# Norm borders that hand on x s + z g, sums inside the last output tile, and gates made in the branch stages, in a five-branch fp32 kernel

## The reference

```
h = rms_norm(x, norm_g); proj = h @ w_in            # z, xbc, dt, lru gate, lru x, q, gates
xbc = silu(causal_dwconv(xbc, conv_w, conv_b)); dt = softplus(dt_raw + dt_bias)
y_ssd = rms_norm((ssd_scan(xs, dt, -exp(a_log), b, c) + xs * d) * silu(z))
y_lru = rg_lru(causal_dwconv(lru_x)) * silu(lru_gate)
y_mem = memory_attention(q, rms_norm(mem), w_kv)
x = rms_norm(x + (gates0 * (y_ssd @ w0) + gates1 * (y_lru @ w1) + gates2 * (y_mem @ w2)) @ w_out, final_g)
for i, branch in enumerate((s5, swa, mla, sgu)):     # swa: 16 heads, window 128; mla: 16 heads, causal
    x = x + rms_norm(branch(rms_norm(x, pre_norm[i])), post_norm[i])
# s5, swa, mla:  (y * silu(z)) @ w_out, y a scan with GLU or an attention; sgu: (u * s * silu(z)) @ w_out
# s5 coefficients: dt = exp(log_dt), exp(lam_re dt), cos and sin of lam_im dt, and quotients of them
```

## Time and profile before

| | |
|---|---|
| device time, three runs | 2221.42, 2221.95, 2225.58 us (median 2221.95) |
| the profiled execution | 2225.19 us, of which the span is 2223.4 us |
| mean granted TensorE clock | 0.955 of full speed |
| PE busy | 2005.2 us, 90% of the span |
| DVE, ACT, POOL busy | 1293.1, 861.0, 455.7 us |
| data moved | 227.96 MB, mean 103 GB/s |

### The profile page before, as it was taken

One profiled execution on the slowest core, in us unless ns is written; L12 is line 12 of the kernel. 1 busy time (PEld: TensorE's weight loads), 2 busy tenths in 40 slices (PEclk: granted clock), 3 DMA queues, 4 the chain that ended last, 5 costly groups with the idle time before them and its releaser, 6 DMA issues.

```text
span 2223.4 us, 24707 instructions
## 1 busy us (share of the span) xinstructions
PE 2005.2 (90%) x9910; PEld 1569.7 (71%) x9910; DVE 1293.1 (58%) x1862; ACT 861.0 (39%) x1247; POOL 455.7 (20%) x386
## 2 busy tenths in 40 slices
PE   6897888999999999999999887989889988789986
PEld 4685765788667888778787765867667755468865
DVE  6986885725539235555537344475486456547374
ACT  4223646412268224322332342355442344444232
POOL 1864100323158403033300100012001010100001
PEclk9998998999999999999999998999999999999998
DMA  3244331234322534334465527211222210123211
GB/s 137 84 147 136 128 120 55 79 116 147 114 92 80 169 116 156 146 112 151 135 156 148 135 80 157 76 57 39 76 93 82 76 38 19 39 76 123 95 57 57
DMA packets 63938, 227.96 MB, mean 103 GB/s; under 512 B 13744, under 2 KB 30800, under 8 KB 43472
## 3 DMA queue, kind: packets, MB, share of 16 engines
q1 hardware_dynamic: 22896, 162.54, 20.9%
q0 software_dynamic: 20240, 48.58, 7.6%
q10 hardware_dynamic: 20688, 15.26, 3.1%
HBM read 208.72 MB, written 17.56 MB: 102 GB/s over the span
## 4 chain that ended last, share of the span: by engine, by line
PE 61%; DVE 11%; ACT 6%; issue 4%; DMA 2%; ACTq 1%; POOL 0%; DVEq 0%
PE bank L482 17%; PE bank L483 17%; PE bank L484 17%; PE bank L481 2%; DVE ring_low L444 1%; ACT ring_high L439 1%; PE bank L3142 1%; ACT swa_s L3046 1%; ACTq L2414 1%; PE bank L3169 1%; DMA ring<-slabs 1%; PE bank L1938 1%; DVE swa_s L2983 1%; DVE lru_x L1852 1%; PE bank L609 1%
## 5 line engine op out<-in xcount | busy, mean ns | idle before, releaser
L482 PE MATMUL bank<-h_high,ring_high 128*128 128x512 f32 x1248 | 508.5, 407 | 46.1 <-DVE h_low L1364 22.2
L444 DVE TENSOR_TENSOR ring_low<-ring,ring_high 128x2048 fp32r<-128x2048 f32 x136 | 329.4, 2423 | 352.8 <-ACT ring_high L439 352.7
L483 PE MATMUL bank<-h_low,ring_high 128*128 128x512 f32 x1248 | 495.3, 397 | 0.0
L484 PE MATMUL bank<-h_high,ring_low 128*128 128x512 f32 x1248 | 494.3, 396 | 0.0
L439 ACT ACTIVATE ring_high<-ring 128x2048 fp32r<-128x2048 f32 x145 | 277.3, 1913 | 518.5 <-PE bank L484 505.9
L482 PEld LDWEIGHTS bank<-h_high,ring_high 128*128 128x128 f32 x1248 | 240.7, 193 | 116.4 <-issue 52.4
L483 PEld LDWEIGHTS bank<-h_low,ring_high 128*128 128x128 f32 x1248 | 240.5, 193 | 53.4 <-issue 4.4
L484 PEld LDWEIGHTS bank<-h_high,ring_low 128*128 128x128 f32 x1248 | 239.8, 192 | 51.8
L482 PE MATMUL bank<-gated_high,ring_high 128*128 128x512 f32 x256 | 106.1, 415 | 25.1 <-issue 18.2
L444 POOL TENSOR_TENSOR ring_low<-ring,ring_high 128x2048 fp32r<-128x2048 f32 x9 | 43.2, 4805 | 366.5 <-ACT ring_high L439 366.5
L483 PE MATMUL bank<-gated_low,ring_high 128*128 128x512 f32 x256 | 103.7, 405 | 0.0
(11 more groups left out here) (519 smaller groups left out, 3807.5 us busy)
## 6 DMA issues: line engine op xcount, KB each, us to landing
ring<-slabs SPq DMA_DIRECT2D x149, 1024.0 KB, 4.8
acs_rows<-acs_rows POOLq DMA_DIRECT2D x16, 512.0 KB, 4.7
s_outputs<-s_ca POOLq DMA_DIRECT2D x4, 1152.0 KB, 7.2
x<-xT SPq DMA_DIRECT2D x2, 2048.0 KB, 8.8
exp_acs<-acs_rows POOLq DMA_DIRECT2D x16, 256.0 KB, 8.8
s_b<-s_br POOLq DMA_DIRECT2D x8, 512.0 KB, 4.3
s_rows<-s_powers POOLq DMA_DIRECT2D x16, 256.0 KB, 6.3
s_inputs<-s_w POOLq DMA_DIRECT2D x8, 512.0 KB, 3.0
```

Of the source, the lines that this page charges most:

```text
L444: dve.tensor_tensor(self.ring_low[:, s % RING, :], self.ring[:, s % RING, :], self.ring_high[:, self.splits_before[s] % AHEAD, :].bitcast( ...
L482: pe.matmul(out, w[0], x[0], start=start, stop=False)
L483: pe.matmul(out, w[0], x[1], start=False, stop=False)
L484: return pe.matmul(out, w[1], x[0], start=False, stop=stop)
```

## The change

- **Columns and coefficients.** The columns are loaded in three pieces, the 96 of the S5 coefficients first; `s5_coefficients` moves from `stage_xbc` into `stage_load`, ahead of the first squares on ACT and of the first sums on DVE.
- **dt's softplus** is cut in pieces at tiles 4, 8, 12 and 16 of `stage_xbc` (before: all at 4, the sums at 9), and ACT makes a slab's high part one tile earlier.
- **Sum in the tile.** The gathered squares of seven tiles are summed by a matmul at k = 5 of the last output tile; only the last square is summed behind it. At the first block's end the whole sum goes behind k = 2 of the S5 layer's first gemm.
- **Borders.** With s the root of z's mean square, the border hands on x s + z g, s being a factor for each token, and not x + z g / s. The next norm takes it out again (eps s^2 in its sum). The reciprocal and eight products that bring x back to size (`invert_on_dve`, `settle_on_dve`) come inside the next stage's entry. After the first block, whose norm has no add, the parts are made before the root.
- **Gates.** `Gate` makes silu(z), the product and both parts tile by tile inside the branch stages: in S5's GLU stage by a sigmoid, in SWA's and MLA's loops by 0.5 z (1 + tanh(z/2)), where DVE's product reads y from the bank instead of ACT's copy; in `stage_sgu` by silu and a product into u. In MLA the calls stand as in SWA, once for two heads.
- **SGU's output** does its first four tiles together, k outermost, with the blocks in that order.
- **The bias** goes to DRAM in 16 copies instead of 128 and is read back by eight skewed transfers.

```diff
+    add("sgu_out", [("d_w_out", span(k * P), span(m * P)) for k in range(KD) for m in range(4)])
+    for m in range(4, KD):
...
+    loaded, cols, s5_cols = C.reserve("loaded", 16), C.reserve("cols_loaded", 32), C.reserve("s5_cols_loaded", 16)
+    s5_act, s5_dve = s5_coefficients(C)
+    a = COL_AT["lam_re"]
+    own = slice(a, a + 96)
...
-            act.dma_start(C.cols[:], io["cols"]).then_inc(cols.sem, 16)
+            act.dma_start(C.cols[:, own], io["cols"][:, own]).then_inc(s5_cols.sem, 16)
+            act.dma_start(C.cols[:, 0:a], io["cols"][:, 0:a]).then_inc(cols.sem, 16)
+            act.dma_start(C.cols[:, a + 96:NCOL], io["cols"][:, a + 96:NCOL]).then_inc(cols.sem, 16)
+            act.wait_ge(s5_cols.sem, s5_cols.base + 16)
+            s5_act(act)
...
-            dve.wait_ge(cols.sem, cols.base + 16)
+            dve.wait_ge(s5_cols.sem, s5_cols.base + 16)
+            s5_dve(dve)
+            dve.wait_ge(cols.sem, cols.base + 32)
...
             def step_sums():
+                log1p_end(C, dve, L.S1[:], L.S2[:], L.S4[:])
...
                 if i == 4:
-                    step_sizes()
-                if i == 9:
+                    dve.wait_ge(dts.sem, dts.at(1))
+                    log1p_ratio(C, dve, L.S1[:], L.S2[:])
+                if i == 8:
+                    log1p_terms(C, dve, L.S2[:], L.S3[:], L.S4[:], 15, 9)
+                if i == 12:
+                    log1p_terms(C, dve, L.S2[:], L.S3[:], L.S4[:], 7, 3)
+                if i == 16:
...
-                if i >= 3:
-                    C.split_high(act, u)
+                if 3 <= i + 1 < len(tiles):
+                    C.split_high(act, tiles[i + 1][0])
...
+    def sum_gathered(self, pe):
         C, u, n = self.C, self.u, len(self.src)
         C.open(pe, u)
         pe.wait_ge(self.summed.sem, self.summed.at(n - 1 - self.split))
-        mm = pe.matmul(C.bank[u.b][:, 0:self.w], C.ones[:], self.total, start=True, stop=not self.split)
+        return pe.matmul(C.bank[u.b][:, 0:self.w], C.ones[:], self.total, start=True, stop=not self.split)
+    def sum_total(self, pe, gathered=False):
+        C, u, n = self.C, self.u, len(self.src)
+        if not gathered:
+            mm = self.sum_gathered(pe)
...
+        if last.add is not None:
+            self.last_root_on_act(act)
...
-            ins = dve.scalar_tensor_tensor(out=last.tmp[i], in0=last.src[i], scalar=last.g(i), in1=last.root, op0=ALU.mult, op1=ALU.mult)
+            if last.add is None:
+                dve.wait_ge(last.squared.sem, last.squared.at(i))
+                ins = dve.tensor_scalar(C.X[:, i, :], C.X[:, i, :], last.g(i), None, ALU.mult)
+            else:
+                dve.wait_ge(self.before.sem, self.before.at(i))
+                ins = dve.tensor_tensor(C.X[:, i, :], C.X[:, i, :], last.root, ALU.mult)
             ins.then_inc(last.scaled.sem, 1)
         def grow(i):
             if last.add is not None:
                 dve.wait_ge(last.scaled.sem, last.scaled.at(i))
-                dve.tensor_tensor(C.X[:, i, :], C.X[:, i, :], last.tmp[i], ALU.add).then_inc(self.grown.sem, 1)
+                dve.scalar_tensor_tensor(out=C.X[:, i, :], in0=last.src[i], scalar=last.g(i), in1=C.X[:, i, :], op0=ALU.mult,
+                                         op1=ALU.add).then_inc(self.grown.sem, 1)
...
-        C.vchain.link(dve, dve.reciprocal(last.root, last.root))
...
+        last = self.last
+        self.C.read(dve, last.u)
+        dve.scalar_tensor_tensor(out=self.total, in0=last.root, scalar=EPS * DM / P, in1=last.root, op0=ALU.mult, op1=ALU.mult)\
+            .then_inc(self.summed.sem, 1)
...
+    def invert_on_dve(self, dve):
+        dve.wait_ge(self.summed.sem, self.summed.at(0))
+        dve.reciprocal(self.last.root, self.last.root).then_inc(self.inverted.sem, 1)
+    def settle_on_dve(self, dve, i):
+        X = self.C.X[:, i, :]
+        dve.wait_ge(self.inverted.sem, self.inverted.at(0))
+        dve.wait_ge(self.lows.sem, self.lows.at(i))
+        dve.tensor_tensor(X, X, self.last.root, ALU.mult).then_inc(self.settled.sem, 1)
...
+                if i == 4:
+                    entry.invert_on_dve(dve)
+                for n in ({4: (0, 1, 2), 5: (3, 4, 5, 6, 7)} if stats else {4: (0,), 5: (1, 2), 6: (3, 4), 7: (5, 6, 7)}).get(i, ()):
+                    entry.settle_on_dve(dve, n)
...
+                        if k == 2:
+                            entry.last.sum_total(pe)
...
+            entry.invert_on_dve(dve)
+            for i in range(KD):
+                entry.settle_on_dve(dve, i)
...
+    def after_glu(act, i):
+        if i + 1 < KD:
+            gate.curve_on_act(act, i + 1, C.zbuf[:, i + 1, :], ACT.Sigmoid, 1.0)
+        if i > 0:
+            gate.high_on_act(act, i - 1)
+        if i == KD - 1:
+            gate.high_on_act(act, i)
     def glu_mul(dve, i):
         dve.tensor_tensor(Y[:, i, :], Y[:, i, :], L.Y[:, i, :], ALU.mult).then_inc(glu_made.sem, 1)
-    glu_tiles = stage_gemm(C, KD, L.G, glu, then=glu_mul, side=Side(ready=split))
+        gate.factor_on_dve(dve, i, C.zbuf[:, i, :], 0.0)
+        dve.wait_ge(glu_made.sem, glu_made.at(i))
+        dve.wait_ge(gate.factor.sem, gate.factor.at(i))
+        dve.tensor_tensor(Y[:, i, :], Y[:, i, :], C.zbuf[:, i, :], ALU.mult).then_inc(gate.mul.sem, 1)
+        if i > 0:
+            gate.low_on_dve(dve, i - 1)
...
+        self.slots = [C.root[:, 1, :]]
...
+    def curve_on_act(self, act, k, z, fn, scale):
+        if k > 0:
+            act.wait_ge(self.factor.sem, self.factor.at(k - 1))
+        act.activation(self.slots[0], z, fn, scale=scale).then_inc(self.curve.sem, 1)
+    def factor_on_dve(self, dve, k, z, plus):
+        dve.wait_ge(self.curve.sem, self.curve.at(k))
+        dve.scalar_tensor_tensor(out=z, in0=self.slots[0], scalar=plus, in1=z, op0=ALU.add, op1=ALU.mult).then_inc(self.factor.sem, 1)
+    def high_on_act(self, act, k):
+        act.wait_ge(self.mul.sem, self.mul.at(k))
+        act.activation(self.parts.high[:, k, :], self.Y[:, k, :], ACT.Copy).then_inc(self.high.sem, 1)
+    def low_on_dve(self, dve, k):
+        dve.wait_ge(self.high.sem, self.high.at(k))
+        dve.tensor_tensor(self.parts.low[:, k, :], self.Y[:, k, :], self.parts.high[:, k, :].bitcast(F32), ALU.subtract)\
+            .then_inc(self.low.sem, 1)
...
+            for u in us:
+                C.open(pe, u)
+            for k, row in enumerate(blocks):
+                pe.wait_ge(gate.low.sem, gate.low.at(k))
+                for u, (s, i) in zip(us, row):
+                    C.wait_slab(pe, s, seen)
+                    mm = C.product(pe, C.bank[u.b][:], C.block(s, i), gate.parts.tile(k), k == 0, k == KD - 1)
+                    if k == KD - 1:
+                        mm.then_inc(C.bank_full[u.b], 1)
...
+                if i >= together:
+                    ready = (lambda k: pe.wait_ge(gate.low.sem, gate.low.at(k))) if i == 0 else None
+                    if i == KD - 1:
+                        ready = lambda k: post.sum_gathered(pe) if k == 5 else None
+                    C.gemm(pe, t, gate.parts.tiles(KD), seen, ready=ready)
                 if i in side.tensor:
                     side.tensor[i](pe)
-            post.sum_total(pe)
+            post.sum_total(pe, gathered=True)
...
-        pool.dma_start(scr, L.BV[:].unsqueeze(1).to_broadcast([16, P, 384])).then_inc(s.sem, 16)
+        pool.dma_start(scr, L.BV[:].unsqueeze(1).to_broadcast([16, 16, 384])).then_inc(s.sem, 16)
         pool.wait_ge(s.sem, s.base + 16)
-        skewed = bass.AP(tensor=scr.tensor, offset=127, ap=[[383, P], [P * 384, 16], [1, 256]])
-        pool.dma_start(L.BT[:], skewed).then_inc(s.sem, 16)
+        for a in range(8):
+            skewed = bass.AP(tensor=scr.tensor, offset=127 - 16 * a, ap=[[383, 16], [16 * 384, 16], [1, 256]])
+            pool.dma_start(L.BT[16 * a:16 * a + 16], skewed).then_inc(s.sem, 16)
...
+            def gated(j):
+                u = ob[j]
+                C.full(dve, u)
+                dve.wait_ge(gate.factor.sem, gate.factor.at(j))
+                dve.scalar_tensor_tensor(out=L.Y[:, j, :], in0=C.bank[u.b][:], scalar=0.5, in1=L.Z[:, j, :], op0=ALU.mult,
+                                         op1=ALU.mult).then_inc(C.bank_read[u.b], 1)
+                C.read(dve, u)
+                dve.sem_inc(gate.mul.sem, 1)
...
+            gate.factor_on_dve(dve, 0, L.Z[:, 0, :], 1.0)
             for j in range(NJ):
                 if j + 1 < NJ:
                     probs(j + 1)
+                if j > 0:
+                    gated(j - 1)
                 if j + 2 < NJ:
                     logits(j + 2)
                     evac_z(j + 2)
+                if j + 1 < NJ:
+                    gate.factor_on_dve(dve, j + 1, L.Z[:, j + 1, :], 1.0)
+                if j > 1:
+                    gate.low_on_dve(dve, j - 2)
+            gated(NJ - 1)
+            for j in (NJ - 2, NJ - 1):
+                gate.low_on_dve(dve, j)
...
+            def curve(j):
```

(53 more changed lines are left out.)

182 lines of the change are left out of this document (101 added, 81 removed).

## The result

The changed kernel takes 2187.18 us (median of 4 runs, 2184.87 to 2193.54), the kernel before 2223.55 (4 runs): a ratio of 0.9841, interval 0.9817 to 0.9865, or 35 us less. The forecast was 2167, some 56 less. The time lies just inside the range of 2150 to 2188, but outside the 2155 to 2180 that had a chance of 0.62, and a third of the forecast gain is missing. The profiled execution took 2188.14 us, its span 2186.0; 37.4 less than the 2223.4 of before.

A forecast was written before the change was run, and what follows sets the result against it. PE, busy for 90% of the span, was taken as the bound, so only its idle time and the lower-clock matmuls after it could be won. The terms sum to -56.4, giving 2167 us; forecast 2155 to 2180, range 2150 to 2188.

The forecast's parts named there:

- Start: Kernel start: split columns load and early S5 coefficients delay PE's first sum, +7.5 us; ends +2 and +8.
- Convolution: First block's convolution and scan: dt's softplus in pieces and POOL's earlier chain remove PE's waits, -20.5 us.
- The other part of the term, the scan: Before the SSD scan: POOL's chain begins some 38 us earlier, so PE's wait of 9.71 goes, -9.4 us.
- its other bound: Convolution and scan: only part is won, -12 us, if POOL is slowed or slows the low halves.
- Border to S5 and S5's gate: First block to S5: reciprocal leaves the path, -6.1 us; S5's output stage starts with only the last k open, -7.6.
- MLA's entry: Entry of MLA: reciprocal and eight settling products, 8.9 us on DVE against 3 idle, +5.2 us; bounds 3 and 6.
- SGU: SGU's output: gate made earlier and first four tiles k-major, ending together near 2174.5, -6.5 us; bounds -4 and -8.
- Borders, gates, loops: Later borders -10.4, -2.6, -2.6; gates of S5, SWA, MLA -7.6, -8.0, -8.2; loops of SWA +6.1, MLA -3.5.
- The slower one: Head loops: DVE's new product waits for PE's attention product, loops run in series; +39, 2261 us; chance 0.03.
- The early landing: Kernel start: the first piece of columns lands early, making the start cheap; -62, 2161 us; chance 0.14.
- this rival: Head loops: tanh has its own table, two loads of 1.28 per 16 tiles, +41; -15, 2207 us; chance 0.02.
- the -34: SWA's and MLA's loops give back more, +25 against +2.6; total -34, 2189 us; chance 0.11, including table loads.

The follow-up runs named there:

- pool_held: The changed kernel with POOL's chain of S5 tables held until the 24th tile of the convolution is done; 2280.54 us.
- coef_back: The changed kernel with the S5 coefficients computed in the convolution's stage as before, columns still in three pieces; 2189.27 us, ratio 0.9849.
- glu_low: The changed kernel with the last low part of S5's gate ahead of the slab's low half, not behind it; 2179.97 us (one run).

## Why the forecast was wrong where it was

- **Start (+7.5, measured +8.2).** Right in mechanism and size: the piece landed at 8.6 and the squares began at 14.68. The Trainium skill (DMA: Bandwidth & Descriptors, Queues, rings and completion order) has the engines take turns between queues packet by packet. The trace agrees (205 packets on one queue and 190 on the other in 9 us). What does not hold is what the forecast drew from it, an early landing and +2 for "a piece with a third of the descriptors": the piece has as many packets as x, 144, and landed with it. What the forecast did not see is that the two other pieces would now hold DVE until 14 by themselves.
- **Convolution (-20.5, measured -12.8).** The step that failed is the sum of won waits, 1.2 + 8.7 + 2.5 + 1.0 less 2.3 for "a wait that I expect at a low half", -11.1. PE's last gemm matmul ahead of the scan (187.16 before, 195.20 after) is 8.0 us late, where the first was 8.2 late: 0.2 us were won. The wait of 8.74 fell to 2.61, but the new one is 5.43, not 2.3, and with the matmuls behind it at a granted clock of 0.64 (166 to 172 us; 1.00 there before) it took 7.5 back. The cover assumed for the pieces was the slack of a slab, 10.9 us of PE for 16 blocks. In fact DVE is busy all through, and POOL, brought forward by the same change, stretches DVE's steps (3.05 for 0.68). Shown by pool_held; coef_back agrees. The other part of the term, the scan, won 12.7 and not 9.4: its wait went, and the matmuls behind it, which ran at a granted clock of 0.52 (197 to 203 us), now have 1.00 (195 to 200), which the forecast left out. coef_back shows that the wait went because POOL's chain starts earlier (33 us, not the 38 of the forecast). The text had -12 as its other bound and chose the wrong end; that the total lies so near to -12 is luck, as neither part does.
- **Border to S5 and S5's gate (-13.7, measured -10.4).** In the gate the step "low(7)", which the working took as free, stood behind a slab's low half and cost 3.5 us (glu_low); without it the gate would have won 9.9, more than its 7.6. At the border PE's first S5 matmul won 5.1 us and the one at 1094.83 6.2, as forecast. Some 2 us are lost again up to 1252, in the part of the span where repeats differ; why was not tried.
- **MLA's entry (+5.2, measured +7.2).** The step was right (no idle time for 8.9 us of DVE), and PE's waits grew by 4.7, from 4.16 to 6.14 and 2.74. The size was off at the clock: the forecast took 0.7 off for it, but the matmuls in and behind the two waits cost 2.5 more (granted clock 0.59 from 1641 to 1654, 0.84 from 1664 to 1675 before).
- **SGU (-6.5, measured -0.4).** The step "k-major the first four end together" left out that four banks must be free. With them free 6.9 more are won.
- **Borders, gates, loops.** Each reciprocal, gate and loop term came out within 1.3 us, apart from the border to SGU, won 1.8 more; there 1.2 of the gain come behind the first matmul, where matmuls at the lower clock (0.63 for 0.39) go on for 6 us in the kernel before and for 3 here. In SWA the new wait sits where the text put it, with the product ahead of the logits, and PE waits for the bank that the product reads. No table loads came with tanh: the two loops have none. The Trainium skill (ScalarE: Activation LUTs, Table sets: the hidden batching unit) has tanh in exp's set, and the trace agrees. "Nothing before runs a tanh" was a misreading: the LRU does (L1867), and there tanh and exp follow each other with no load between (647.01 to 652.21), so that a row of before could have settled this rival. Its price was also set against the forecast (-15) and not against the -34 that it was said to come on top of.
- **The rivals.** The slower one did not come: DVE waited for PE's attention product 0.2 us in all in SWA's loop. The early landing did not come either, until x was held back.

## What to carry to other kernels

When an edit starts POOL's work earlier, look at what DVE does in that stretch: beside POOL a step of DVE on SBUF took up to four times as long (3.05 for 0.68), and a DVE without idle time passes it on. When a load is cut in pieces, count the packets of each piece and not its bytes. When a loop order is changed so that several tiles are open at once, check which banks they get and who still reads them. A step that is moved off the end of a chain has to be checked for whether it was on it: the sum of the gathered tiles ran beside the last square, and moving it into the tile cost 0.85 us a border.

## What the runs showed that was not expected

- A transfer's wait depended on what shares the engines with it and on packets, far more than on its size: 12 KB, third in its queue, took 12.4 us beside x and the slabs and 2.1 alone, 48 KB 7.8 and 1.8, while the load of x took 7.6 and 7.4.
- DVE's operations that read a PSUM bank kept their length beside POOL (the three steps of the convolution, 2.32 us with and without it), and so did the reciprocal of 32x512 (3.34), while others from SBUF to SBUF grew: 0.68 to 3.05, 2.28 to 3.84 for a slab's low half. Why these and not the reciprocal was not tried.
